# Encoder layer on one Trainium2 core: a mixture-of-experts' down matrices fetched in one transfer, with four hidden rows to a partition

## The reference

```python
def block(args):
    xb, e = args
    g, u = jnp.split(xb @ w_gu[e], 2, axis=-1)     # w_gu[e]: 2048 x 1024
    return (jax.nn.silu(g) * u) @ w_d[e]           # w_d[e]: 512 x 2048
...
x = x + g2 * hierarchical_moe(hf, ...)
return rms_norm(x, final_g)
```

## Time and profile before

| | us |
|---|---|
| median of 3 runs | 1490.36 (1488.64 to 1490.91) |
| the profiled execution, its own time | 1486.37 |
| its span in the profile | 1484.5 |
| TensorE busy | 1155.1 (78%) |
| VectorE busy | 633.9 (43%) |
| ScalarE, GpSimd busy | 175.2, 95.5 |

### The profile page before, as it was taken

One profiled execution on the slowest core, in us unless ns is written; L12 is line 12 of the kernel. 1 busy time (PEld: TensorE's weight loads), 2 busy tenths in 40 slices (PEclk: granted clock), 3 DMA queues, 4 the chain that ended last, 5 costly groups with the idle time before them and its releaser, 6 DMA issues.

```text
span 1484.5 us, 20553 instructions
## 1 busy us (share of the span) xinstructions
PE 1155.1 (78%) x8500; PEld 737.7 (50%) x8500; DVE 633.9 (43%) x1026; ACT 175.2 (12%) x395; POOL 95.5 (6%) x122
## 2 busy tenths in 40 slices
PE   4999999999999998767577578568558558657655
PEld 4788888888888884333233125124214224223222
DVE  5667768777747524552132123124114114214214
ACT  3011242221134120300000000000000000000002
POOL 3111101111100000000000000000000000000001
PEclk9999999999999999979789878889779879888877
DMA  8999999999996477999999999999999999999996
GB/s 317 383 387 388 399 376 383 386 393 384 319 374 240 164 299 318 427 413 410 428 428 427 430 428 428 430 428 428 430 428 428 430 428 428 430 428 427 429 428 246
DMA packets 116139, 577.92 MB, mean 389 GB/s; under 512 B 10250, under 2 KB 51296, under 8 KB 90484
## 3 DMA queue, kind: packets, MB, share of 16 engines
q1 hardware_dynamic: 89572, 474.37, 78.6%
q0 software_dynamic: 26512, 102.77, 18.0%
HBM read 575.02 MB, written 2.10 MB: 389 GB/s over the span
## 4 chain that ended last, share of the span: by engine, by line
PE 49%; DMA 42%; DVE 5%; issue 1%; SPq 1%; ACT 1%; DVEq 0%; ACTq 0%
DMA ring<-in_moe_w_gu_dram 27%; PE psum L1147 8%; PE psum L739 7%; DMA ring<-in_moe_w_d_dram 7%; DMA ring<-in_da_w_in_dram 7%; PE psum L775 5%; PE psum L1054 5%; PE psum L1176 4%; PE psum L749 4%; PE psum L1199 3%; PE psum L965 3%; PE psum L886 2%; PE psum L878 2%; PE psum L711 1%; SPq L435 1%
## 5 line engine op out<-in xcount | busy, mean ns | idle before, releaser
L1147 PE MATMUL psum<-ring,ada_ring 128*32 128x256 f32 x3696 | 277.8, 451 | 145.8 <-DMA ring<-in_moe_w_gu_dram 145.8
L1147 PEld LDWEIGHTS psum<-ring,ada_ring 128*32 128x32 f32 x3696 | 125.8, 121 | 292.1 <-DMA ring<-in_moe_w_gu_dram 193.2
L1176 PE MATMUL psum<-ring,arena 128*32 128x512 f32 x960 | 157.0, 801 | 25.9 <-ACT arena L1444 16.0
L1975 DVE TENSOR_SCALAR arena<-arena 128x128 f32<-128x128 f32 x32 | 7.3, 227 | 353.2 <-ACT arena L1438 353.2
L1992 DVE TENSOR_TENSOR arena<-psum,arena 32x512 f32<-32x512 f32 x108 | 74.2, 687 | 186.0 <-PE psum L1176 176.2
L775 PE MATMUL psum<-region_b,ring 128*128 128x256 f32 x512 | 117.6, 389 | 6.7 <-DMA ring<-in_da_w_in_dram 3.7
L739 PE MATMUL psum<-region_b,ring 128*128 128x256 f32 x512 | 112.0, 379 | 0.0
L775 PEld LDWEIGHTS psum<-region_b,ring 128*128 128x128 f32 x512 | 98.7, 195 | 22.2 <-issue 4.4
L739 PEld LDWEIGHTS psum<-region_b,ring 128*128 128x128 f32 x512 | 96.8, 190 | 12.7
L1438 ACT ACTIVATE arena<-psum 128x128 f32<-128x128 f32 x32 | 8.9, 277 | 784.8 <-PE psum L1147 740.3
L1525 DVE SCALAR_TENSOR_TENSOR arena<-ada_ring,silu_c,arena 128x512 f32<-128x512 f32 x120 | 90.2, 752 | 22.3 <-DMA ada_ring<-in_ada_w_dram 18.6
(11 more groups left out here) (271 smaller groups left out, 1120.1 us busy)
## 6 DMA issues: line engine op xcount, KB each, us to landing
ring<-in_moe_w_gu_dram SPq DMA_DIRECT2D x123, 2048.0 KB, 25.7
ring<-in_moe_w_d_dram SPq DMA_DIRECT2D x62, 2048.0 KB, 24.5
ada_ring<-in_ada_w_dram POOLq DMA_DIRECT2D x88, 1024.0 KB, 10.9
ring<-in_da_w_in_dram SPq DMA_DIRECT2D x15, 2048.0 KB, 38.7
ring<-in_da_w_in_dram SPq DMA_DIRECT2D x18, 1024.0 KB, 26.0
ring<-in_da_w_out_dram SPq DMA_DIRECT2D x8, 2048.0 KB, 19.9
ada_ring<-in_ada_w_dram POOLq DMA_DIRECT2D x16, 512.0 KB, 12.7
ring<-in_moe_w_d_dram SPq DMA_DIRECT2D x8, 512.0 KB, 18.1
```

The lines of the kernel that those rows point to most:

```text
L1147: last = mm(psum[32 * n:32 * n + 32, B_GU, 0:256].rearrange("p (a b) -> p a b", a=2), x_items[:, k, SLOTS * i:SLOTS * (i + 1)], w[:, :, n ...
L1176: last = mm(psum[32 * n:32 * n + 32, B_D + i % 2, :], hid_t[:, k, :], w[:, kk, n, :], start=k == 0, stop=k == FT - 1)
```

## The change

From item 1 on (`down_in_one`; item 31 stays in eight pieces) the down matrix comes as one transfer of 4 MB, with 32 KB in a row per partition, into the two neighbouring slots, which `dma_start` sees as one stretch. It waits for the later of the two slots, and signals once, on the first slot's semaphore. TensorE waits for it ahead of part 4 and not again at part 5. Each partition now holds four neighbouring rows of `w_d` (feature 4 q + kk), for item 0 in two transfers. `hidden_tiles` and its users follow: the moving columns of L1147 (now L1163), L1070 and `spare_gu` are now four elements apart.

```diff
         def w_d(e):
-            return moe_w_d[0, bass.ds(e, 1), :, :].rearrange("e (j p kk) n -> p (e j) (kk n)", p=P, kk=2)
+            return moe_w_d[0, bass.ds(e, 1), :, :].rearrange("e (p kk) n -> p e (kk n)", p=P, kk=FT)

         def hidden_tiles(rows):
-            return rows.rearrange("p (two j q kk) -> p two j kk q", two=2, j=2, kk=2)
+            return rows.rearrange("p (two q kk) -> p two kk q", two=2, kk=FT)
...
+        DOWN_PAIR = moe_slot(None, 5)
+
+        def down_in_one(m):
+            return not isinstance(m, int) or m > 0
+
         def moe_loads(m, j):
+            if moe_slot(m, j) == DOWN_PAIR and down_in_one(m):
+                return 1 + whole_loads(moe_at(m, j))
             return m + whole_loads(moe_at(m, j))
...
-                    sp.wait_ge(w_used, slot_free(m, turn))
+                    if j == 5 and down_in_one(m):
+                        continue
+                    in_one = j == 4 and down_in_one(m)
...
+                    sp.wait_ge(w_used, slot_free(m, turn + 1 if in_one else turn))
...
+                    elif in_one:
+                        sp.dma_start(ring[:, s:s + 2, :].rearrange("p (j s) x -> p j (s x)", j=1), dn)\
+                            .then_inc(w_loaded[s], 16)
                     else:
                         sp.dma_start(ring[:, s, :].rearrange("p (j x) -> p j x", j=1),
-                                     dn[:, j - 4:j - 3, :]).then_inc(w_loaded[s], 16)
+                                     dn[:, :, CH * (j - 4):CH * (j - 3)]).then_inc(w_loaded[s], 16)
...
-            dn = moe_w_d[0, EXPERTS - 1, :, :].rearrange("(j p kk) n -> p j kk n", p=P, kk=2)
+            dn = moe_w_d[0, EXPERTS - 1, :, :].rearrange("(p j kk) n -> p j kk n", p=P, kk=2)
...
-                                              x_items[:, k, SLOTS * i:SLOTS * (i + 1)], w[:, :, n // 2, n % 2, :],
+                                              x_items[:, k, SLOTS * i:SLOTS * (i + 1)], w[:, :, n, :],
...
-                        s = moe_slot(m, j)
                         w = ring[:, s, :].rearrange("p (k n f) -> p k n f", k=2, n=4)
-                        pe.wait_ge(w_loaded[s], moe_loads(m, j) * 16)
+                        if j == 4 or not down_in_one(m):
+                            pe.wait_ge(w_loaded[s], moe_loads(m, j) * 16)
```

More of the change, by code:

```diff
@@ L361, in spare_gu @@
             rows = spare_halves[i][k // 2][:, 1024 * (k % 2):1024 * (k % 2 + 1)]
-            return hidden_tiles(rows)[:, :, n // 2, n % 2, :]
+            return hidden_tiles(rows)[:, :, n, :]
         def feature_quad(row, k):
@@ L467, in load_item @@
                         continue
-                    sp.wait_ge(w_used, slot_free(m, turn))
+                    if j == 5 and down_in_one(m):
+                        continue
+                    in_one = j == 4 and down_in_one(m)
+                    assert not in_one or not isinstance(m, int) or slot_free(m, turn) <= slot_free(m, turn + 1)
+                    sp.wait_ge(w_used, slot_free(m, turn + 1 if in_one else turn))
                     s = moe_slot(m, turn)
@@ L1081, in last_two @@
                         w = ring[:, s, :].rearrange("p (k n f) -> p k n f", k=2, n=4)
-                        pe.wait_ge(w_loaded[s], moe_loads(m, FIRST_DOWN + j) * 16)
+                        if j == 0:
+                            pe.wait_ge(w_loaded[s], moe_loads(m, FIRST_DOWN) * 16)
                         for kk in range(2):
@@ L1148, in moe_group @@
                                           x_items[:, k, SLOTS * i:SLOTS * (i + 1)],
-                                          w[:, :, n // 2, n % 2, :] if spare is None else spare_gu(spare, kk, n),
+                                          w[:, :, n, :] if spare is None else spare_gu(spare, kk, n),
                                           start=k == 0, stop=k == KT - 1)
```

## The result

| | before | with the change |
|---|---|---|
| median of five runs, us | 1490.46 (1488.64 to 1491.37) | 1534.72 (1531.86 to 1537.97) |
| ratio | | 1.0307 (95%: 1.0292 to 1.0323) |
| the profiled execution, us | 1486.37 | 1537.97 |

The change costs 3.1%, 44 us. I had said 1516.9 and a range of 1500 to 1531: right in sign, too low by 18 us and outside the range. Between the two profiled executions the difference is 51.6 us, since one lies 4.1 under its median and the other 3.3 over it.

A forecast was written before the change was run, and what follows sets the result against it. It took TensorE to bound group 0 and the 428 GB/s transfer stream to bound the rest. 24.2 + 2.3 + 2.0 - 2.0 = +26.5 us took the profiled 1486.37 to 1512.9, median 1516.9, range 1500 to 1531.

The forecast's parts named there:

- Part 1, the rate: Products with moving columns four apart: a round takes about twice as long, a part 3.73 us instead of 1.87.
- Rival 1: Distance four costs nothing in the ring: not slower, 1492 us, with bounds 1488 to 1494; no separate chance given.
- Part 1, group 0: Slower products in group 0 delay item 5's first part, so the stream starts again 24.2 us later.
- Group 1's first item: Part and gather take 5.7 us against 4.90 for a transfer, so holes appear in the stream: +2.3 us.
- The six seams: Between later groups the queue lasts until TensorE's next issues: zero cost, 0 to 0.6 us for the range.
- Part 4: Rows of 32 KB save packets in 30 pairs: 0 to 3.7 us gained, half taken, -2.0 us.
- ten transfers deep from T on: At a seam, the queue after the last pair's landing at T runs dry at T + 49.0.
- the prediction's 1.7 us: A transfer issued into an empty queue starts to move data about 1.7 us after its issue.
- Part 2, SP's wait: SP's one wait for the later slot: a 3.9 us later start that vanishes behind the slower products; nothing in steady regime.
- Part 3, TensorE's wait: Down product starts only when both halves have landed: covered inside a group, +2.0 us at the end (item 30).
- Rival 3: Group 0 as forecast, but 32 KB rows slow the stream by half a per cent: +4.5 us, 1523; chance 0.05.
- Rival 2: TensorE becomes the bound, a group taking 120 us against 117.5: about +50 us, 1540; chance 0.06.

The follow-up runs named there:

- e12: e1 with the moving columns in neighbouring pairs (rows of four and two transfers kept): 1497.53 us.
- e1: Changed kernel with the down matrix in two 2 MB transfers again and the waits as before; rows of four and distance four kept: 1515.58 us.
- e9: Changed kernel with moving columns in neighbouring pairs, four 64x64 products turning the gate's result, and the 4 MB transfer for items 4 to 29 only: 1496.83 us.
- e5: e1 with SP issuing both halves only after the later slot's wait, TensorE still waiting for each half apart: 1514.60 us.
- e8: e3 with two transfers for items 1 to 3 and 30, the 4 MB transfer for items 4 to 29 only; doesn't compute the layer: 1487.24 us.
- e3: Changed kernel with moving columns two apart as before; 32 KB rows, 4 MB transfer and joint waits kept; doesn't compute the layer: 1498.23 us.
- e2: Changed kernel with the old rows and columns: one 4 MB transfer in two runs of 16 KB per partition, joint waits kept: 1500.11 us.

## Why the prediction was wrong, step by step

**Part 1, the rate: right.** 632 ns against the 624 read from L636, and 3.67 us a part in group 0 (14.69 / 4) against 3.73. The row of another line with the same stride told it. Rival 1, that distance four is free, is out, and with it, for this operand, the second half of what the prediction quotes from the Trainium skill, page "SBUF — State Buffer", section "Door 1: The DMA port swizzle (why [64,N] ≈ [32,N])": four float32 elements of stride aren't free here, 632 ns for 388. e12 against e1 closes the question of why: with the same rows, transfers and buffer, two neighbours per quad give 389 ns (388 in e9) and one element per quad gives 632. The Trainium skill, page "Advanced Engine Details and Errata", section "SBUF Cachelines", says that a line of 16 bytes needs two hits or more for full performance. The traces agree: one hit at distance four, two at distance two and with pairs.

**Part 1, group 0: right, a little low.** +26.5 for +24.2, down product of item 2 +24.7 for +22.3. The clock gave nothing back: item 0's down product took 5.19 and item 1's rose from 3.64 to 5.34, and the first gather from 3.84 to 5.18. Why the clock was lower in these last two, although TensorE was busier, is open.

**Group 1's first item: right**, +2.6 for +2.3.

**The six seams: the step that failed**, "I take zero, with 0 to 0.6 us at six seams". It was worth 18.4 us, 20.4 with the 2.0 of Part 4 that lie in the same stretch, of the 25.1 us between my sum and the profile. Two things were wrong in it: the queue was taken as too deep, and TensorE's way to its next issues as too short. A third was left out, that the other issues behind T meet the queue as well.

First, the queue's side. I let it be "ten transfers deep from T on", where T is the moment TensorE sees the pair. But a transfer is seen landed after its last byte moved, while the next is already moving. The times from issue to landing of two transfers issued into an empty queue, the pair issued at 574.48 and the part issued at 694.57, show it:

```profile
L489 SPq DMA_DIRECT2D ring<-in_moe_w_d_dram x1: 328/328/328, 574.5 to 574.5; - x1
...
DMA to landing us min/median/max: 13.3/13.3/13.3
```

```profile
L486 SPq DMA_DIRECT2D ring<-in_moe_w_gu_dram x1: 333/333/333, 694.6 to 694.6; - x1
...
DMA to landing us min/median/max: 8.1/8.1/8.1
```

At 428 GB/s their bytes need 9.8 and 4.9 us, so 3.5 and 3.2 us are something else. With the prediction's 1.7 us ahead of the data, 1.5 to 1.8 us are left behind the last byte. This is an estimate, and the stream in steps of 0.25 us bears it out for the part: its first packets move 0.9 to 1.2 us after the issue, slowly at first, its 2.1 MB are through by about 701.3, and it is seen landed at 702.7. So the queue runs dry near T + 47.4, not T + 49. The Trainium skill, page "DMA: Bandwidth & Descriptors", section "Anatomy of one DMA — SWDGE (gpsimd) path", puts a fixed cost of some 2 us mostly behind the last byte. That is stated for GpSimd's path, and on SP's queue the 1.5 to 1.8 us behind the last byte estimated here are of that size, with about as much again ahead of the data.

Second, TensorE's side came out just over my span. The pair's issue is at 838.28, T + 47.7, and its data would move from T + 49.4 on. I had 45.5 to 49 for that moment. Two terms put it there: the whole down product after T at the lower clock, 5.69 us where e1 has some 1.9 left, and the first gather behind it, 5.46 us where I had 3.8. The gather takes as long in e1, so only the first of the two comes of the joint wait. And the pair isn't the closest place, as I had it. The group's first part already meets it: issued at T + 25.9 (816.41), moving from T + 27.6, when the six transfers ahead of it end at T + 29.4 - 1.7 = T + 27.7. From there on TensorE takes a gather and a part in 5.7 us against 4.9 for a transfer, so the next two issues are later still. Walked through with these times, the queue stands empty for 0.7 and 0.8 us ahead of the second and third part and for 0.6 ahead of the pair: 2.1 us. From landing to landing of a group's last pair (790.55 to 1395.08, five groups) a group takes 120.9 us for the 117.5 of the stream, so 2.1 of 3.4 us have a place. Without the joint wait all is some 4 us earlier: e1 issues that first part at 809.76, with T at 787.94, T + 21.8. With fast products it is earlier by nearly two microseconds for each part. Either margin is enough, and that is why the table above has large holes in one corner only. That the dips follow from these margins is read from the issue times. The table itself shows only that it takes both. How much of the 4 us is the lower clock and how much the later start was not separated, and where the other 1.3 us of a group are lost is open.

**Part 2, SP's wait: right.** It vanishes (e5 against e1: 1514.60 and 1515.58).

**Part 3, TensorE's wait: right place, wrong size, and not the only place.** The end cost 4.1 for 2.0: the down product behind the landing took 6.59 us where 2.47 were left, behind a wait of 3.39 us for the pair. It stands at the lower clock, as at the seams. "Inside a group that is covered" holds (e8), but a group's last item isn't inside one, and neither is group 0. With fast products group 0 loses some 7 us to it (e3), which in the changed kernel is hidden behind the slower TensorE. Rival 1's time of 1492 would have been wrong for that reason even with a free distance: e2 and e3, which are that kernel, took 1500.11 and 1498.23.

**Part 4, 32 KB rows: right**, -1.9 (e3 against e2) for -2.0. SP's queue moves 85,252 packets in e3 and 89,092 in e2, the 30 x 128 fewer that the term counted. That half of the 3.7 us came out is luck: I had no better reason for a half. Rival 3 is out.

**Rival 2**, TensorE as the bound with 120 us a group, gave 1540 and so came nearest by number, with the wrong mechanism. Groups do take 119.7 to 122.6 us from first gather to first gather, where before had 116.8 to 117.8 after group 1. But TensorE isn't short over a group: between seams it idles before each part (1.10 us at 780.75), and the stream is full (431 GB/s). It is short for some 30 us behind each seam. I had priced the rival as a sum over the group and so thrown it out by the average, and the same average let me take zero in the forecast. I should have walked through the seam issue by issue.

## What to carry to other kernels

A change to a transfer's layout is first a change to how the matrix engine reads: look for another line with the same stride and take its record. When a wait is merged, look not at the mean slack but at the place where the engine restarts behind the wait, and walk the next issues one by one against the queue, counted from the last byte's move and not from its semaphore. Two margins that each hold alone can fail together, and only a two-by-two of runs shows that.

## What the runs showed of the hardware

- A float32 product of 128x256 moving columns has a record of 632 ns with one element used in 16 bytes, and 388 ns with two, whether the two are neighbours or 8 bytes apart.
- A transfer on SP's queue into an empty queue needed 3.2 us (2 MB) and 3.5 us (4 MB) more than its bytes at 428 GB/s. In a full queue this doesn't show: over 700 to 1400 the stream has 428 GB/s with all transfers of 2 MB (before) and with the down matrices in 4 MB (e2). Rows of 32 KB instead of 16 KB for a third of the bytes gained 1.9 us in some 900.
- At all six seams of the changed kernel and at its end TensorE idled 3.2 to 3.4 us ahead of the down product, and the product took 5.0 to 5.7 us and 6.6 at the end in place of 3.64. At the first seam the granted clock was 1.00 ahead of the wait and 0.50 behind it. Such a wait isn't the only cause: item 9's product (855.96) took 5.34 behind an idle of 0.56 us.
